# Prompt attention in 16 steps of two heads with softmax in place, and gates in quarters by tanh

## The chip, the cores and the metric

The kernel runs on one core of a Trainium2 chip. The metric is the device time of one execution in microseconds (us). Three runs of the kernel before took 1583.16, 1587.78 and 1589.92 us; the median is 1587.78.

## The reference

One decoder layer for two groups of tokens that share weights: a prompt of 512 tokens and 64 sample tokens (8 sequences of 8), 1024 channels. The layer is half a SwiGLU feed-forward (width 2816), a combined input projection that feeds a convolution branch and a sparse attention branch, a merge by two sigmoid gates, an output projection and another half feed-forward. What matters here, cut to its core:

```python
# h = rms_norm(x); q, k, v: 8 heads x 64; u: 512 channels for the convolution
gate_c, gate_a = sigmoid(gc), sigmoid(ga)              # 1024 channels each

def gathered_attention(q, k_sel, v_sel, valid):
    logits = einsum('thd,tkhd->thk', q, k_sel) * 64 ** -0.5
    logits = where(valid[:, None, :], logits, -inf)
    p = softmax(logits, axis=-1)
    return einsum('thk,tkhd->thd', p, v_sel)

def merge_branches(x, conv_out, att, gate_c, gate_a, w_aout, w_o):
    a = att.reshape(B, T, 512) @ w_aout
    return x + (gate_c * conv_out + gate_a * a) @ w_o
```

For the prompt, the keys of a token are the 128 best of the causal ones by an indexer score; for a sample token they are 256 of 4096 cached ones, gathered from HBM. The convolution is causal, depthwise and 31 wide.

## The kernel before

All is fp32. Activations lie transposed, channels on partitions and the 576 tokens (64 sample, 512 prompt) along the free dimension; 576 columns are done as two halves of 288 (HALF) in two PSUM banks. The order of work on each engine is written out by hand, and engines are tied by semaphores. DMA queues hold the weights: SP loads w_in in tiles of 512 KB into six slots (`wn`), and tile m is loaded when tile m-6 has been used (`native_load`, on the semaphore ring_used).

The stage that the change touches begins after the 14 mixing units (`mix_unit`) that compute a part of the input projection. Its parts are interleaved:

Prompt attention. 32 steps, four blocks of 128 queries times eight heads. Block b has 128 (b+1) keys. In step i TensorE computes the logits of head i (`plogits`, bank 5, contraction over the 64 rows of the head, 64 h mod 128 being the first row), VectorE adds a bias that masks the keys not selected, finds the extremum and writes to Lp (`prompt_mask`, L2495), ScalarE takes exp into Pp with the sum of the row (`pexp`, L1695), VectorE takes the reciprocal (`prompt_quotient`), ScalarE scales (`pscale`, L1701), TensorE transposes (`pturn`, L1222, bank 6) two steps later, ScalarE copies to pTp (`pevac`, L1708), TensorE multiplies by the values (`pvalue`, L1232, bank 7, 64 columns of the array) three steps after the logits, and ScalarE copies out every second head (`pout`).

Gates. The last ten weight tiles, 14 to 23, give five of the eight pairs of gate rows; each tile holds half of the contraction. `gate_half` (L1198) does 8 matmuls of 288 columns on one tile and one of two groups m of output rows, at the 20 steps of HALF_AT, into banks 0 to 3. ScalarE applies Sigmoid (`gate_low`, L1681, `gate_high`, L1686), and `save_gate` stores the 1152 columns to HBM.

Sample attention values. `values(n)` (L1094) multiplies gathered value rows of value n in four column parts of 32, into bank 4; values 11 to 31 run in steps 0 to 20. GpSimd gathers them, four indirect DMAs per value, into three buffers (`gather_values`, L2719): gather n may start when value n-3 has been used. ScalarE prepares the weights (`fill`), VectorE masks the result of each eight (`own_heads`). In step 24 come `new_values` and `group_out`, small products.

Convolution. VectorE does one of the 31 taps per step (`conv_tap`, L2530, four instructions of 512 columns) and eight pieces of the sample's (`conv_sample`). When the last is done, TensorE sums over channels (`conv_sums`, L1241, banks 1 and 2), which ends the stage; then follow the merging units (`unit`, L592) with the gates' multiplications in VectorE (`gate`), the output projection and the second feed-forward.

Of the kernel before, what the change touches and what calls it, by code (L numbers as in the profile page):

```python
# [23 lines left out]
P = 128  # L24
# [82 lines left out]
def hybrid_step(nc, inp, con, out):  # L107
    ctx = ExitStack()
    with ctx:  # L109
# [121 lines left out]
        (pTp, gpack), e_ = place(used["iT"][0], [("pTp", (P, 2, 4, P), F32), ("gpack", (P, KC, NS), F32)])  # L231
        assert e_ <= used["wisc"][0]
        (Lp, Pp, mzb), e_ = place(used["h_hi"][0], [("Lp", (P, 2, SEQ), F32), ("Pp", (P, 4, SEQ), F32), ("mzb", (P, 2, DA), F32)])
# [93 lines left out]
        STEP_0 = 11  # L327
        FILL_AT = {2 * b - STEP_0 - 2: b for b in range(7, 16)}
        HEADS_AT = {8 * g + 8 - STEP_0: g for g in range(1, 4)}
        V_SLOT, V_SEM, V_KEYS = (4, 0, 2), (4, 5, 0), (60, 62, 64)  # L330
        HALF_AT = (0, 2, 3, 4, 6, 8, 9, 10, 12, 14, 15, 16, 18, 20, 22, 24, 25, 26, 28, 30)
# [240 lines left out]
        def _(pe):  # L572
# [616 lines left out]
            def gate_half(n, m):  # L1189

                if m == 0:
                    pe.wait_ge(S_(f"ring{(NB + n) % RING}"), native_count(NB + n))
                if n % 2 == 0:
                    pe.wait_ge(S_("mix_free" if m else "sgb_ready"), n // 2 - 2)
                wt = wn[:, SLOT[(NB + n) % 6], :].rearrange("p (k n) -> p k n", k=4)
                for k in range(4):
                    for hf_ in range(2):
                        mm = pe.matmul(ps[:, 2 * m + hf_, 0:HALF], wt[:, k, m * P:(m + 1) * P],  # L1198
                                       h32[:, 4 * (n % 2) + k, hf_ * HALF:(hf_ + 1) * HALF],
                                       start=(n % 2 == 0 and k == 0), stop=(n % 2 == 1 and k == 3))  # L1200
                if m == 1:
                    mm.then_inc(S_("ring_used"), 1)
                elif n % 2 == 1:
                    mm.then_inc(S_("gate_part"), 1)

            steps = [(b, h) for b in range(4) for h in range(H)]

            def plogits(i):
                b, h = steps[i]
                r = 64 * (h % 2)  # L1210
                if i >= 1:
                    pe.wait_ge(S_("plog_used"), i)
                pe.matmul(ps[:, 5, 0:P * (b + 1)], qTp[r:r + 64, h // 2, P * b:P * (b + 1)], kTp[r:r + 64, h // 2, 0:P * (b + 1)],
                          start=True, stop=True).then_inc(S_("plog_done"), 1)

            def pturn(i):
                b, h = steps[i]
                pe.wait_ge(S_("pprob_ready"), i + 1)
                if i >= 1:
                    pe.wait_ge(S_("pturn_evac"), i)  # L1220
                for kb in range(b + 1):
                    mm = pe.transpose(ps[:, 6, kb * P:(kb + 1) * P], Pp[:, i % 4, kb * P:(kb + 1) * P], ident[:, :])  # L1222
                mm.then_inc(S_("pturn_done"), 1)

            def pvalue(i):
                b, h = steps[i]
                r = 64 * (h % 2)
                pe.wait_ge(S_("pturn_evac"), i + 1)
                if i >= 2 and i % 2 == 0:
                    pe.wait_ge(S_("patt_evac"), i // 2)  # L1230
                for kb in range(b + 1):
                    mm = pe.matmul(ps[r:r + 64, 7, 0:P], vnp[:, kb, h * HD:(h + 1) * HD], pTp[:, i % 2, kb, :],  # L1232
                                   start=(kb == 0), stop=(kb == b))
                mm.then_inc(S_("patt_done"), 1)
# [9 lines left out]
            for i in range(len(steps) + 3):  # L1244
                if i < len(steps):
                    plogits(i)
                if i in HALF_AT:
                    q = HALF_AT.index(i)
                    gate_half(N_MIX + q // 2, q % 2)
                if 2 <= i <= len(steps) + 1:  # L1250
                    pturn(i - 2)
                if i >= 3:
                    pvalue(i - 3)
                if i + STEP_0 < 32:
                    values(i + STEP_0)
                if i == 24:
# [4 lines left out]
                if i == 34:  # L1261
                    pe.wait_ge(S_("mix_free"), 10)
                    conv_sums(0, yacc)
# [24 lines left out]
        def _(act):  # L1288
# [295 lines left out]
            def sigmoid(half):  # L1584

                for m in range(2):
                    act.activation(halves(sgb[:, m, :]), pair_ps(half, m), ACT.Sigmoid).then_inc(S_("sgb_ready" if m == 0 else "mix_free"), 1)  # L1587
# [33 lines left out]
            def save_gate(i):  # L1621

                act.wait_ge(S_("sgb_ready"), i + 3)
                act.wait_ge(S_("mix_free"), i + 3)
# [52 lines left out]
            def gate_low(i):  # L1677

                act.wait_ge(S_("gate_part"), i - 2)
                act.wait_ge(S_("gate_saved"), 16 * i + 16)  # L1680
# [36 lines left out]
            for i in range(35):  # L1717
                if i < 32:
                    pexp(i)
# [1104 lines left out]
```

## Time and profile before

| | |
|---|---|
| median of three runs | 1587.78 us (1583.16 to 1589.92) |
| span of the profiled execution | 1586.6 us |
| PE (TensorE) | 1484.6 us busy, 94% |
| DVE (VectorE) | 1104.5 us, 70% |
| ACT (ScalarE) | 499.6 us, 31% |
| POOL (GpSimd) | 585.4 us, 37% |
| read from and written to HBM | 237.58 MB and 10.20 MB |

The profile is of one execution. Busy time of an engine is the union of its instructions; waits on semaphores aren't in it. Starts of matmuls are recorded, their ends are modelled. PEld is the loading of weights into the array. The granted clock is a share of 2.4 GHz. A releaser is inferred from semaphore events; "issue" means that no releaser was found, "remote" that it wasn't an engine's instruction that the trace can name.

### The profile page before, as it was taken

What the parts mean: (1) busy time and instruction counts of PE and PEld (TensorE: products, weight loads), DVE (VectorE), ACT (ScalarE), POOL (GpSimd) and SP (SyncE); (2) the same over time, 40 slices, a digit from 0 to 9 for tenths busy, and PEclk for the clock granted to TensorE, in tenths of its full rate; (3) what the DMA queues carried; (4) which work ended last, traced back from release to release, by engine and by line L of the source; (5) the groups of instructions that cost most, each with busy time, mean ns of one, the idle gap of its engine ahead of it and who ended that gap; (6) DMA issues with size and microseconds to landing.
All of it is one profiled execution on the core that took longest, in us unless ns stands there. A gap on an engine that the chain in (4) does not pass through costs nothing. (4 is left out here: it accounts for less than half of the span.)

```text
span 1586.6 us, 20793 instructions
## 1 busy us (share of the span) xinstructions
PE 1484.6 (94%) x8219; PEld 1147.5 (72%) x8219; DVE 1104.5 (70%) x1680; ACT 499.6 (31%) x756; POOL 585.4 (37%) x412
## 2 busy tenths in 40 slices
PE   5989999899999989999899789999999999999998
PEld 2323488677888865446666445669999999999998
DVE  1357399999985898999996676565679865565221
ACT  2233322112112222121212344464346544453221
POOL 2001264443338865554245775013120645520000
PEclk9998999999999999999999898999999999999999
DMA  9994153222226888868458776023422332222222
GB/s 343 389 381 161 50 85 113 93 80 80 80 80 221 286 276 276 290 213 278 125 163 269 222 237 187 17 101 126 138 75 68 93 107 82 92 68 74 74 87 93
DMA packets 156931, 248.77 MB, mean 157 GB/s; under 512 B 11965, under 2 KB 104909, under 8 KB 156571
## 3 DMA queue, kind: packets, MB, share of 16 engines
q1 hardware_dynamic: 131742, 164.22, 32.0%
q0 software_dynamic: 23104, 76.16, 15.4%
q10 hardware_dynamic: 1989, 7.07, 1.1%
q8 instruction: 64, 1.05, 0.3%
q14 instruction: 32, 0.26, 0.0%
HBM read 237.58 MB, written 10.20 MB: 156 GB/s over the span
## 5 line engine op out<-in xcount | busy, mean ns | idle before, releaser
L2651 POOL TENSOR_TENSOR w_lo<-w_raw,w_hi 128x1024 fp32r<-128x1024 f32 x65 | 165.5, 2546 | 294.8 <-ACT w_hi L1303 294.6
L686 PE MATMUL ps<-bh,wqr 128*128 128x288 f32 x936 | 205.3, 295 | 4.2 <-DVE wqr L1843 2.0
L1303 ACT ACTIVATE w_hi<-w_raw 128x1024 fp32r<-128x1024 f32 x88 | 91.5, 1040 | 314.7 <-PE ps L637 231.5
L2707 POOL DMA_INDIRECT kv<-cache_k,idxT x128 | 142.2, 1111 | 81.4 <-DVE kprod L2356 48.9
L2719 POOL DMA_INDIRECT kv<-cache_v,idxT x128 | 134.7, 1052 | 99.3 <-PE ps L1094 47.0
L686 PEld LDWEIGHTS ps<-bh,wqr 128*128 128x128 f32 x936 | 155.5, 188 | 5.0 <-DVE wqr L1843 3.9
L637 PE MATMUL ps<-h_hi,w_hi 128*128 128x512 f32 x352 | 139.2, 395 | 2.8 <-POOL w_lo L2651 1.5
L637 PE MATMUL ps<-h_lo,w_hi 128*128 128x512 f32 x352 | 137.7, 391 | 0.0
L637 PE MATMUL ps<-h_hi,w_lo 128*128 128x512 f32 x352 | 137.7, 391 | 0.0
L1079 PE MATMUL ps<-h,wn 128*128 128x288 f32 x448 | 115.5, 417 | 8.1 <-ACT sgb L1587 4.6
L702 PE MATMUL ps<-a_hi,wqr 128*128 128x288 f32 x704 | 122.3, 295 | 0.0
L686 PE MATMUL ps<-bl,wqr 128*128 128x288 f32 x384 | 113.3, 295 | 0.0
L1079 PEld LDWEIGHTS ps<-h,wn 128*128 128x128 f32 x448 | 86.2, 195 | 37.0 <-ACT sgb L1587 6.2
L1044 PE MATMUL ps<-wn,xg 128*128 128x512 f32 (+1 forms) x256 | 103.2, 563 | 5.0 <-DVE xT L2175 3.0
L702 PEld LDWEIGHTS ps<-a_hi,wqr 128*128 128x128 f32 x704 | 103.1, 188 | 0.0
L1856 DVE TENSOR_TENSOR wqr<-wq,wqr 128x1024 fp32r<-128x1024 f32 (+1 forms) x24 | 27.2, 1135 | 95.2 <-ACT wqr L1341 95.2
L1044 PEld LDWEIGHTS ps<-wn,xg 128*128 128x128 f32 x256 | 49.7, 196 | 56.2 <-issue 47.1
L1198 PE MATMUL ps<-h,wn 128*128 128x288 f32 x320 | 88.3, 432 | 0.7 <-ACT sgb L1686 0.7
L2356 DVE TENSOR_TENSOR kprod<-kv,qb 128x1024 f32<-128x1024 f32 x64 | 81.9, 1280 | 8.5 <-issue 3.1
L2775 POOL TENSOR_TENSOR wq<-wq 128x1024 f32<-128x1024 f32 x10 | 24.9, 2490 | 170.4 <-PE ps L686 76.7
L637 PE MATMUL ps<-a1h,w_hi 128*128 128x512 f32 x176 | 71.6, 407 | 14.8 <-DVE w_lo L1812 7.5
L1198 PEld LDWEIGHTS ps<-h,wn 128*128 128x128 f32 x320 | 62.6, 201 | 27.2 <-issue 8.7
(493 smaller groups left out, 3268.9 us busy)
## 6 DMA issues: line engine op xcount, KB each, us to landing
w_raw<-w_ffn_in SPq DMA_DIRECT2D x56, 512.0 KB, 13.1
wq<-w_ffn_in SPq DMA_DIRECT2D x40, 512.0 KB, 3.6
wn<-w_in SPq DMA_DIRECT2D x36, 512.0 KB
qb<-q_scratch SPq DMA_DIRECT2D x64, 256.0 KB
ring<-w_ffn_in SPq DMA_DIRECT2D x28, 512.0 KB
w_raw<-w_ffn_out SPq DMA_DIRECT2D x24, 512.0 KB, 10.1
wq<-w_ffn_out SPq DMA_DIRECT2D x20, 512.0 KB
ring<-w_ffn_out SPq DMA_DIRECT2D x14, 512.0 KB
```

Source lines behind the costliest of these rows:

```text
L637: mm = pe.matmul(ps[:, 2 * half + m, :], w[:, k, m * P:(m + 1) * P], x[:, kc0 + k, c0:c0 + SEQ], start=(first and k == 0 and fst), stop=(l ...
L686: mm = pe.matmul(ps[:, bank + m, 0:HALF], w[:, k, m * P:(m + 1) * P], b[:, j, k, :], start=(j in (0, 1, 5) and k == 0 and fst), stop=(k == ...
L702: mm = pe.matmul(ps[:, 4 * half + 2 * m + hf_, 0:HALF], w[:, k, m * P:(m + 1) * P], x[:, kc0 + k, hf_ * HALF:(hf_ + 1) * HALF], start=(kc0 ...
L1044: mm = pe.matmul(ps[:, s % 8, 0:n], xg[:, kk, P * b:P * b + P], wt[:, k, :], start=(kk == 0), stop=(kk == KD - 1))
L1079: mm = pe.matmul(ps[:, 4 * half + 2 * m + hf_, 0:HALF], wt[:, k, m * P:(m + 1) * P], h32[:, 4 * (n % 2) + k, hf_ * HALF:(hf_ + 1) * HALF], ...
L1198: mm = pe.matmul(ps[:, 2 * m + hf_, 0:HALF], wt[:, k, m * P:(m + 1) * P], h32[:, 4 * (n % 2) + k, hf_ * HALF:(hf_ + 1) * HALF], start=(n % ...
L1303: act.activation(w_hi[:, slot, 0:n], w_raw[:, slot, 0:n], ACT.Copy).then_inc(S_("hi_ready"), 1)
L1856: dve.tensor_tensor(wqr[:, 6 + o % 2, 0:n], wq[:, 8 + o % 2, 0:n], wqr[:, 4 + o % 2, 0:n].bitcast(F32), ALU.subtract).then_inc(S_("lo_read ...
L2356: dve.tensor_tensor(kprod[:, :, :], kv[:, n % KV, :, :], qb[:, j, :].unsqueeze(1).to_broadcast([P, 2, DA]), ALU.mult)\
L2651: pool.tensor_tensor(w_lo[:, slot, 0:n], w_raw[:, slot, 0:n], w_hi[:, slot, 0:n].bitcast(F32), ALU.subtract)\
L2707: pool.indirect_dma_start(kv[:, n % KV, c, :], None, rows[0], bass.IndirectOffsetOnAxis(ap=idxT[:, c, n:n + 1], axis=0))\
L2719: pool.indirect_dma_start(kv[:, V_SLOT[j % 3] + a // 2, a % 2, :], None, rows[1], bass.IndirectOffsetOnAxis(ap=idxT[:, j % 2, t:t + 1], ax ...
```

## The change

The prompt attention goes in 16 steps of two heads. Logits of the two heads are issued one behind the other, on rows 0 to 63 and 64 to 127 of the array, into banks 5 and 6. Mask, exp and scaling all work in one buffer, Pp, with three places of two heads; Lp is gone. The two value products alternate between columns 0 to 63 and 64 to 127 for each block of keys. Transposes go to banks 2 and 3. TensorE's order in a step is logits j, values j-2, one gate quarter, transposes j-1, the other quarters of the step, sample values. Two convolution taps are done per step.

Gates are computed in quarters, 8 matmuls over the whole contraction for one of two groups of rows and one half of the columns, from both tiles of a pair, alternately into banks 0 and 1; the last is in step 13. ScalarE applies tanh(x/2) in the place of the sigmoid, in all eight pairs. The merge restores it: (tanh + 1) times the branch, and a factor 0.5 in the splitting of the merged rows.

```diff
-        STEP_0 = 11
+        QUARTERS = ((0, 1), (2,), (3,), (4, 5), (6,), (7,), (8, 9), (10,), (11,), (12, 13), (14,), (15,), (16, 17), (18, 19))
+        VALUES = ((11, 12), (13,), (14, 15), (16,), (17, 18), (19,), (20, 21), (22,), (23,), (24, 25), (26, 27), (28,), (29, 30), (31,))
...
+            def gate_quarter(q):
+
+                n, m, hf_ = N_MIX + 2 * (q // 4), q % 4 // 2, q % 2
+                if q % 4 == 0:
+                    for t in (n, n + 1):
+                        pe.wait_ge(S_(f"ring{(NB + t) % RING}"), native_count(NB + t))
+                if q < 2:
+                    pe.wait_ge(S_("mix_free"), 5)
+                else:
+                    pe.wait_ge(S_("gate_taken"), q - 1)
+                for k in range(KD):
+                    wt = wn[:, SLOT[(NB + n + k // 4) % 6], :].rearrange("p (k n) -> p k n", k=4)
+                    mm = pe.matmul(ps[:, hf_, 0:HALF], wt[:, k % 4, m * P:(m + 1) * P], h32[:, k, hf_ * HALF:(hf_ + 1) * HALF],
+                                   start=(k == 0), stop=(k == KD - 1))
+                    if q % 4 == 3 and k % 4 == 3:
+                        mm.then_inc(S_("ring_used"), 1)
...
+            def plogits(j):
+
+                b, hp = j // 4, j % 4
+                nk = P * (b + 1)
+                if j >= 1:
+                    pe.wait_ge(S_("plog_used"), 2 * j)
+                for h in range(2):
+                    r = 64 * h
+                    mm = pe.matmul(ps[:, 5 + h, 0:nk], qTp[r:r + 64, hp, P * b:P * (b + 1)], kTp[r:r + 64, hp, 0:nk], start=True, stop=True)
+                mm.then_inc(S_("plog_done"), 1)
...
+                for kb in range(b + 1):
+                    for h in range(2):
+                        r = 64 * h
+                        mm = pe.matmul(ps[r:r + 64, 7, 0:P], vnp[:, kb, (2 * hp + h) * HD:(2 * hp + h + 1) * HD], pTp[:, (2 * j + h) % 3, kb, :],
+                                       start=(kb == 0), stop=(kb == b), skip_group_check=True)
...
+            for j in range(18):
+                if j < 16:
+                    plogits(j)
+                if j >= 2:
+                    pvalue(j - 2)
+                if j < len(QUARTERS):
+                    gate_quarter(QUARTERS[j][0])
+                if 1 <= j <= 16:
+                    pturn(j - 1)
+                if j < len(VALUES):
+                    for q in QUARTERS[j][1:]:
+                        gate_quarter(q)
+                    for n in VALUES[j]:
+                        values(n)
+                if j == 14:
+                    pe.wait_ge(S_("mz_ready"), 4)
+                    new_values()
...
+                if j == 17:
+                    pe.wait_ge(S_("gate_taken"), 20)
+                    pe.wait_ge(S_("pturn_evac"), 32)
                     conv_sums(0, yacc)
```

ScalarE and VectorE:

```diff
-                sigmoid(0)
+                sigmoid(0, ACT.Tanh, 0.5)
...
+                act.activation(sgb[:, m, hf_ * HALF:(hf_ + 1) * HALF], ps[:, hf_, 0:HALF], ACT.Tanh, scale=0.5).then_inc(S_("gate_taken"), 1)
...
+            for j in range(18):
+                if 1 <= j <= len(QUARTERS):
+                    for q in QUARTERS[j - 1]:
+                        gate_evac(q)
+                if j == 2:
                     act.wait_ge(S_("kv_out"), 16 * 12)
+                if j >= 2:
+                    pout(j - 2)
+                if j < 16:
+                    pexp(2 * j)
+                    pexp(2 * j + 1)
+                if 1 <= j <= 16:
+                    pevac(2 * j - 2)
+                    pevac(2 * j - 1)
+                if j < 16:
+                    pscale(2 * j)
+                    pscale(2 * j + 1)
...
-                dve.wait_ge(S_("plog_done"), n + 1)
+                if n % 2 == 0:
+                    dve.wait_ge(S_("plog_done"), n // 2 + 1)
+                    if n >= 6:
+                        dve.wait_ge(S_("pturn_done"), n - 4)
...
+            for j in range(16):
+                if j in HEADS_AT:
+                    own_heads(HEADS_AT[j])
+                if j == 2:
+                    dve.wait_ge(S_("unat_out"), 32)
+                for h in range(2):
+                    prompt_mask(j // 4, 2 * j + h, (2 * j + h) % 4)
...
+                conv_tap(2 * j)
+                for h in range(2):
+                    prompt_quotient(2 * j + h, (2 * j + h) % 4)
+                if j < 15:
+                    conv_tap(2 * j + 1)
+                if j < 8:
+                    conv_sample(j // 2, j % 2)
...
-                    ins = dve.tensor_tensor(halves(g[:, m, :]), halves(g[:, m, :]), pair_ps(1 - v % 2, m), ALU.mult)
+                    ins = dve.scalar_tensor_tensor(out=halves(g[:, m, :]), in0=halves(g[:, m, :]), scalar=1.0, in1=pair_ps(1 - v % 2, m), op0=ALU.add, op1=ALU.mult)
```

## Rows read from the trace of the kernel before

**Rows 1.** The page: the span, and TensorE's busy time with its share and instructions.
```profile
span 1586.6 us, 20793 instructions
...
PE 1484.6 (94%) x8219; PEld 1147.5 (72%) x8219; DVE 1104.5 (70%) x1680; ACT 499.6 (31%) x756; POOL 585.4 (37%) x412
```

**Rows 2.** Stretches: length, busy time and instructions of each engine, clock, DMA, GB/s.
```profile
868.90:1063.41 194.51, 175.52 (x844) 107.71 (x840) 128.64 (x255) 86.26 (x184) 84.85 (x81) 0.93 0.50 153
...
950.00:960.00 10.00, 9.14 (x31) 5.23 (x32) 8.89 (x16) 2.82 (x9) 6.83 (x7) 0.66 0.60 172
```

**Rows 3.** Waits from 868.9 to 1063.41: who for whom, us, times, longest.
```profile
DVE Lp L2495 <- PE ps L1213: 30.2, 11, 7.6
DVE Lp L2495 <- remote: 23.3, 9, 5.8
```

**Rows 4.** Timeline, TensorE: start, length (us), line, tiles, shapes, count.
```profile
961.25 0.70 PE L1213 MATMUL ps<-kTp,qTp 64*128 64x256 f32 x2
961.87 4.15 PE L1198 MATMUL ps<-h,wn 128*128 128x288 f32 x16
965.86 0.38 PE L1222 MATMUL ps<-ident,Pp 128*128 128x128 f32 x2
966.17 0.65 PE L1232 MATMUL ps<-pTp,vnp 128*64 128x128 f32 x4
966.75 1.06 PE L1094 MATMUL ps<-kv,zq 128*32 128x512 f32 x8
967.74 0.91 PE L1213 MATMUL ps<-kTp,qTp 64*128 64x384 f32 x2
```

**Rows 5.** Timeline, TensorE, near the end of the stage.
```profile
1052.46 0.60 PE L1222 MATMUL ps<-ident,Pp 128*128 128x128 f32 x4
1052.99 1.09 PE L1232 MATMUL ps<-pTp,vnp 128*64 128x128 f32 x8
1054.01 1.12 PE L1213 MATMUL ps<-kTp,qTp 64*128 64x512 f32 x2
1055.07 0.66 PE L1222 MATMUL ps<-ident,Pp 128*128 128x128 f32 x4
```

**Rows 6.** Timeline, TensorE, from the small products to the logits behind them.
```profile
1014.58 0.68 PE L1130 MATMUL ps<-pnT,vns 64*64 64x64 f32 x16
...
1019.26 1.22 PE L1213 MATMUL ps<-kTp,qTp 64*128 64x512 f32 x1
```

**Rows 7.** Timeline, TensorE: indexer logits of four heads on 32 rows each.
```profile
668.40 0.71 PE L1021 MATMUL ps<-iT 32*128 32x256 f32 x8 [0.73 <-ACT iT L1557]
```

**Rows 8.** Timeline, VectorE: masks (L2495), taps (L2530), sample convolution (L2538).
```profile
873.46 0.27 DVE L2495 CUSTOM_DVE_ANT_0 Lp<-ps,causal 128x128 f32<-128x128 f32 x1
...
942.47 1.19 DVE L2538 TENSOR_TENSOR G<-U_s,wconv 128x992 f32<-128x992 f32 x1
...
945.15 0.41 DVE L2495 CUSTOM_DVE_ANT_0 Lp<-ps,bias_new 128x256 f32<-128x256 f32 x1
...
945.49 2.74 DVE L2530 SCALAR_TENSOR_TENSOR yacc<-U_p,wconv,yacc 128x512 f32<-128x512 f32 x4
...
1046.08 0.69 DVE L2495 CUSTOM_DVE_ANT_0 Lp<-ps,bias_new 128x512 f32<-128x512 f32 x1 [0.52 <-PE ps L1213]
```

**Rows 9.** Timeline: GpSimd's gathers and two waits of TensorE's sample values.
```profile
872.34 0.94 POOL L2719 DMA_INDIRECT kv<-cache_v,idxT  x1 [0.30 <-issue]
...
877.75 1.32 PE L1094 MATMUL ps<-kv,zq 128*32 128x512 f32 x8 [2.87 <-issue]
...
950.86 1.93 PE L1094 MATMUL ps<-kv,zq 128*32 128x512 f32 x8 [2.85 <-issue]
```

**Rows 10.** Groups by form, ScalarE, 868 to 1056: count, busy us, mean ns, idle.
```profile
L1695 ACT ACT_TABLE_LOAD x10 | 12.8, 1283 | 6.7 <-issue 5.2 <-ACT sgb L1686 1.5
...
L1695 ACT ACTIVATE Pp<-Lp,small 128x384 f32<-128x384 f32 x8 | 4.9, 616 | 12.5 <-DVE small L2495 12.5
```

**Rows 11.** Timeline, TensorE: the first convolution sums and their wait.
```profile
1063.41 0.75 PE L1241 MATMUL ps<-yacc,ones 128*128 128x288 f32 x2 [0.87 <-ACT sgb L1686]
```

More of the change, by code:

```diff
@@ L1187, in _ @@
             pe.wait_ge(S_("us_state"), 3 + 2 * KC)
[L1189 to L1203, printed above, removed]
-                    mm.then_inc(S_("gate_part"), 1)
@@ L1225, in pvalue @@
[L1225 to L1233, printed above, removed]
+            def gate_quarter(q):
[13 more added lines that the diff above has]
+                        mm.then_inc(S_("ring_used"), 1)
+                if q % 4 < 3:
+                    mm.then_inc(S_("gate_part"), 1)
@@ L1583, in _, with sigmoid @@
                     act.activation(dst[:, b, :], ps[:, (4 * g + b) % 8, 0:n], ACT.Copy, scale=rcol[:, b:b + 1]).then_inc(S_("nat_evac"), 1)
-            def sigmoid(half):
+            def sigmoid(half, func=ACT.Sigmoid, scale=1.0):
                 for m in range(2):
-                    act.activation(halves(sgb[:, m, :]), pair_ps(half, m), ACT.Sigmoid).then_inc(S_("sgb_ready" if m == 0 else "mix_free"), 1)
+                    act.activation(halves(sgb[:, m, :]), pair_ps(half, m), func, scale=scale).then_inc(S_("sgb_ready" if m == 0 else "mix_free"), 1)
             def fill(b):
@@ L1621, in save_gate @@
             def save_gate(i):
-                act.wait_ge(S_("sgb_ready"), i + 3)
-                act.wait_ge(S_("mix_free"), i + 3)
+                if i < 3:
+                    act.wait_ge(S_("sgb_ready"), i + 3)
+                    act.wait_ge(S_("mix_free"), i + 3)
+                else:
+                    act.wait_ge(S_("gate_taken"), 4 * (i - 2))
                 act.dma_start(gate_dram[i:i + 1, :, :].rearrange("o p n -> p (o n)"), sgb[:, :, :].rearrange("p m n -> p (m n)"))\
@@ L2573, in _ @@
                     dve.wait_ge(S_("us_state"), 2 * KC + 1)
[L2574 to L2578 removed]
+                conv_tap(2 * j)
+                for h in range(2):
+                    prompt_quotient(2 * j + h, (2 * j + h) % 4)
[3 more added lines that the diff above has]
+                    conv_sample(j // 2, j % 2)
+                if j == 15:
                     sample_heads()
@@ L2606, in gate @@
                         dve.wait_ge(S_("parts_hi"), KA + KC + 2 * (v - 4) + m + 1)
-                        dve.tensor_tensor(m_lo[:, 2 * (v - 4) + m, :], g[:, m, :], m_hi[:, 2 * (v - 4) + m, :].bitcast(F32), ALU.subtract)\
+                        dve.scalar_tensor_tensor(out=m_lo[:, 2 * (v - 4) + m, :], in0=g[:, m, :], scalar=0.5, in1=m_hi[:, 2 * (v - 4) + m, :].bitcast(F32), op0=ALU.mult, op1=ALU.subtract)\
                             .then_inc(S_("m_ready"), 1)
```

142 lines of the change are left out of this document (50 added, 92 removed).

## The prediction

> **What bounds the kernel now.** The page says where to look: TensorE (PE) is busy 94% of the span of 1586.6 us [rows 1], so time comes out where PE has less to do or waits less. The change touches only the prompt-attention stage, which PE enters with the first logits at 868.90 us and leaves when the convolution sums start at 1063.41. The table of stretches shows 194.51 us there, PE busy 175.52, so 19.0 us idle, and a mean granted clock of 0.93 [rows 2]. The clock has two levels, 2.4 and 1.2 GHz; a mean of 0.93 is 14% of the stage, 27 us, at the lower one, where each us does half a us of work: 13.6 us lost. One low stretch is seen between 950 and 960, where the mean is 0.66 [rows 2]. VectorE (DVE) is busy 128.64 of the 194.51, ScalarE (ACT) 86.26, GpSimd (POOL) 84.85 [rows 2]: none fills the stage, but DVE is next. After the stage PE goes on to matmuls of prepared weights that it runs nearly without a gap, so I count a stage shortened by x as a kernel shortened by x. DVE waits with its mask for PE's logits 30.2 us in 11 waits, and 23.3 us in 9 more whose releaser the trace doesn't name [rows 3]: the engines hand small tasks to and fro 32 times.
>
> **PE's work before, by starts.** Ends of matmuls are modelled, so I price each piece from its start to the next start. From the middle of the stage [rows 4]: logits of 256 keys 0.62 us (961.25 to 961.87), half a gate 3.99, two transposes 0.31, values of two key blocks 0.58, sample values 0.99. From its end [rows 5]: four transposes 0.53, values of four blocks 1.02, logits of 512 keys 1.06. So 128 more keys cost 0.22 in logits, 0.22 in values and 0.11 in transposes, whose start alone costs 0.09. Each block of queries has eight heads:
> logits 8 x (0.40+0.62+0.84+1.06) = 23.4; values 8 x (0.36+0.58+0.80+1.02) = 22.1; transposes 8 x (0.20+0.31+0.42+0.53) = 11.7; gates 20 x 3.99 = 79.8; sample values 11 to 31, 21 x 0.99 = 20.8; the small products of new_values and group_out 4.7 (1014.58 to 1019.26) [rows 6]. Sum 162.5. With 13.6 of clock and 19.0 idle that is 195.1 against the measured 194.5: the account closes.
>
> **The change, part by part.** *Two heads at once.* The two logits use rows 0 to 63 and 64 to 127 and go to banks 5 and 6; the two value products use columns 0 to 63 and 64 to 127 of one bank. The trace has both kinds of side-by-side work: four matmuls of 32 rows and 256 keys (an fp32 matmul shows as two records) took 0.71 us together [rows 7], as much as the one of 64 rows (0.70) [rows 4], and the sample values, four column parts of 512 elements, take 0.99 in all [rows 4], about one alone. So I price a pair as one head: logits 4 x 2.92 = 11.7 (-11.7), values 4 x 2.76 = 11.0 (-11.1). The bounds are 0 and the full halves. Transposes use the whole array and only share their start: 4 x (0.31+0.53+0.75+0.97) = 10.2 (-1.5). Gates in quarters are the same 8 matmuls per piece, 79.8; sample values 20.8 (seven follow another directly and may be 0.1 shorter, not counted); small products 4.7. Sum 138.2, which is 24.3 less.
>
> *Waits, by walking the 16 steps.* PE's step j is logits j, values j-2, a gate quarter, transposes j-1, the other quarters, sample values; by the prices above 9.8, 5.7, 6.9, 9.9, 7.1, 6.5, 11.4, 6.7, 6.9, 11.9, 8.2, 7.4, 12.2, 11.6, 7.9 (with the small products), 3.3, 2.2 and 1.0 us. Logits j+1 need DVE's two masks of step j, transposes j the scaling in ACT of step j, with a whole step between. DVE's step is two masks (0.41 us at 256 keys, 0.69 at 512), two taps at 2.74 and in the first eight steps one sample convolution with its reciprocal, 2.68 from 942.47 to the next mask at 945.15 [rows 8]: 8.7 to 9.0 us in the first eight steps, 6.3 to 6.9 later. It starts at 873.46, as before, after the last key selection [rows 8], and passes 943 to 944 us at the start of step 8, where PE asks for logits 9 at about 943: 1 us of wait. From there PE has more per step. POOL issues a value's four gathers at 0.94 us each with 0.30 between, 5.0 us at best [rows 9], and I take 5.3, and a gather may start only when the value three before it is used. Value 12's last gather ended at 873.28 and PE started value 12, after 2.87 idle, at 877.75: 4.4 us of landing [rows 9]. With that, value 12 now comes after two quarters and is there; value 15 comes right behind 14 at 890.9 but lands at about 894 (3.3 us of wait); value 27 costs 1.4. At the end transposes 15 wait for DVE's tap 30 and the scaling behind it, 2.9. Idle by the walk 8.5. Before, several of the 19.0 have no cause I can name (the 23.3 us of unnamed releasers are their other side [rows 3]); handshakes are halved and most have slack, so I add 3: 11.5 instead of 19.0 (-7.5). Bounds: 8.5 and 19.
>
> *The clock.* The low stretch after 950 came with a wait of 2.85 us at 950.86, and the wait at 877.75 was as long [rows 2, 9]. A wait of this length remains at value 15, one at the end, and the small products with 16 columns stay. I take 10 of 13.6 (-3.6); bounds 3 and 13.6, with nothing measured that would make it worse, since PE idles less.
>
> *Tanh for sigmoid, banks of their own.* ACT loads its function table ten times ahead of exp, at 1283 ns each [rows 10], and as often on the way back to sigmoid: 25.7 us of an engine 44% busy. The convolution sums wait 0.87 us for the last sigmoid [rows 11]. The last quarter now runs in step 13, so this goes; it is in the idle sum above. Whether tanh and exp share a table no row shows. If they do, ACT loses all but at most one load and nothing more falls on the path, because PE does not wait for exp in the walk.
> The Trainium skill says that they do: "ScalarE: Activation LUTs", section "Table sets: the hidden batching unit", lists tanh in the set of exp, and also in that of sigmoid; no run here shows it yet.
>
> *Edits at nothing.* A quarter waits for ACT's copy two quarters back (gate_taken); transposes and sample values are queued behind it, but the copy is at the head of ACT's previous or present step. Weights: a tile of the pair is released at the fourth quarter, so SP's loads of tiles 36 and 37 start at about 889 instead of right behind the halves, for use at 944; the cover is 50 us. Tile 31 is wanted at 869 instead of 887; its load is issued during the mixing units, ahead of the stage. DVE's wait for transposes three steps back, and for unat_out in step 2, is for work long done. Merging gains 24 scalar_tensor_tensor in place of tensor_tensor; a tap of that form on 512 elements takes 0.69 us, as does the mask that reads PSUM [rows 8], so the form costs little: 0 to 0.1 us each, beside PE's units, 0 to 1 us in all.
>
> The sum: -24.3 - 7.5 - 3.6 = -35.4. Of the profiled 1586.6 that leaves 1551.2; the median of the runs, 1587.78, is 1.2 above the span, so 1552 us.
>
> **The rivals.**
> 1. *Waits and clock stay as they were* (32.6 us): only the work goes, 1563. For it: part of the idle has no named cause. Against: fewer, slacker handshakes.
> 2. *DVE becomes the bound.* Its work is 15.4 in masks, 84.9 in 31 taps, 21.4 in samples, some 3 in the rest, 125 us from 873.5, ending at 998; if it still waited the 53.5 us that the masks wait now [rows 3], the stage would end near 1052: 12 saved, 1576. Against: it lags behind PE in the first nine steps and has nothing to wait for.
> The Trainium skill has this as a rule: "TensorEngine Tiling (Array Packing)", section "PSUM Bottleneck", says that tiling speeds up TensorE but not the emptying of PSUM, which may become the limit; before the change the trace shows no such limit, with DVE busy for 66% of the stage.
> 3. *The row halves don't overlap*: 11.7 back, 1564. [rows 7] speaks against it.
> 4. *Tanh has another table than exp*: two loads at each of 14 groups of quarters, 36 us of ACT; half of them ahead of exp, 18 us, of which slack hides two thirds: 6 on the path, 1558.
> 5. *The walk holds exactly* and the clock loses 3: -24.3 - 10.5 - 10.6, 1542.
> 6. *Slower: the step's chain is not hidden.* With ACT's passes at the 0.62 us of exp on 384 keys [rows 10]: logits 0.84, masks 1.1, exp 0.6, the tap ahead of the reciprocal 2.9, scaling 1.2, transposes 0.75, copy 0.6, values 0.8, 8.8 us. If the in-order queues left only gates and sample values (100.6 in 16 steps, 6.3 each) outside it, a step would take 15.1 us and sixteen 242, against 194.5: 1635. It decides from 12.2 us per step. The order by code puts one step between mask and transposes and another before the values, which speaks against.
>
> **How the numbers follow.** Forecast 0.50; rival 1 0.17; 2 0.08; 3 0.04; 4 0.06; 5 0.11; 6 0.04. 1552 is the likeliest case; alone it would span 1546 to 1559. The range 1537 to 1571 takes in rivals 1, 3, 4 and 5 and leaves out 2 and 6. About 0.5% (8 us) is what a measurement can tell from no change: faster than 1580 in all cases but 6 and the worst of 2, so 0.94; within 0.02; slower 0.04.
>
> **What would show it.** Pairs of logits of 512 keys at about 1.1 us from start to next start, value pairs of four blocks at 1.0: else rival 3. No or one table load in the stage: else rival 4. The convolution sums start at 1025 to 1030 with PE idle 10 to 13 us and a mean clock of 0.93 to 0.96. A wait at value 15 near 891. Masks that wait for logits in the first nine steps would show DVE ahead, not behind. Wrong would be: PE idle over 19 us, or a stage that ends later than 1040.

## The result, and the profile after

The changed kernel takes 1549.12 us (median of 4 runs, 1545.92 to 1551.51), the kernel before beside it 1585.68 us (4 runs, 1583.16 to 1589.92). The ratio is 0.976, with a 95% interval of 0.9736 to 0.9788. Forecast were 1552 us and a range of 1537 to 1571. The page of the changed kernel, span and busy time, as [rows 1]:

```profile
span 1548.8 us, 20748 instructions
...
PE 1459.2 (94%) x8219; PEld 1136.7 (73%) x8219; DVE 1101.8 (71%) x1680; ACT 472.6 (31%) x746; POOL 586.4 (38%) x412
```

PE is busy 25.4 us less, by as many matmuls. The table of stretches (columns as in [rows 2]) for the stage, for the only two stretches in it with a lower clock, and for what follows the stage:

```profile
869.49:1024.11 154.62, 141.90 (x845) 91.18 (x841) 126.25 (x256) 58.98 (x174) 87.01 (x81) 0.98 0.64 204
890.00:900.00 10.00, 6.83 (x36) 3.07 (x35) 9.86 (x19) 2.79 (x11) 6.83 (x7) 0.83 0.94 328
1010.00:1020.00 10.00, 9.01 (x77) 7.41 (x76) 9.17 (x21) 6.48 (x15) 2.43 (x1) 0.83 0.71 269
1024.11:1204.00 179.89, 172.10 (x1222) 167.89 (x1220) 131.88 (x122) 83.69 (x110) 43.03 (x17) 0.98 0.30 98
```

The stage went from 194.5 to 154.6 us, which is 39.9 less; it starts 0.6 later, and the rest of the kernel behind it takes 524.7 us instead of 523.2; so the span falls by 37.8. A mean clock of 0.83 over 10 us is 3.4 us at 1.2 GHz instead of 2.4, which costs half of it, 1.7; the two stretches together cost 3.4 us. Behind the stage, in the stretch with 0.98, the clock is low twice for about 3.4 us, from 1127.6 and from 1199.6; the kernel before has no low clock from 1063 to 1250.

TensorE's pieces from the timeline, to be read from start to next start, as [rows 4], [rows 5] and [rows 6]: pairs of 256, 384 and 512 keys, a wait at a sample value, waits at values, and the end of the stage:

```profile
895.50 1.88 PE L1096 MATMUL ps<-kv,zq 128*32 128x512 f32 x8 [3.17 <-DMA kv<-cache_v,idxT]
...
908.00 0.70 PE L1218 MATMUL ps<-kTp,qTp 64*128 64x256 f32 x4
908.64 0.44 PE L1244 MATMUL ps<-pTp,vnp 128*64 128x128 f32 x4
...
963.37 0.92 PE L1218 MATMUL ps<-kTp,qTp 64*128 64x384 f32 x4
964.21 0.88 PE L1244 MATMUL ps<-pTp,vnp 128*64 128x128 f32 x12
...
1006.87 1.13 PE L1218 MATMUL ps<-kTp,qTp 64*128 64x512 f32 x4
1007.93 1.09 PE L1244 MATMUL ps<-pTp,vnp 128*64 128x128 f32 x16
1008.95 1.09 PE L1232 MATMUL ps<-ident,Pp 128*128 128x128 f32 x8
1009.97 0.68 PE L1132 MATMUL ps<-pnT,vns 64*64 64x64 f32 x16
1010.59 1.96 PE L1105 MATMUL ps<-qsel,mz 128*128 128x16 f32 x16
1012.39 1.94 PE L1105 MATMUL ps<-qsel,mzb 128*128 128x16 f32 x16
...
1020.23 1.09 PE L1244 MATMUL ps<-pTp,vnp 128*64 128x128 f32 x16 [1.22 <-ACT pTp L1726]
...
1023.08 1.09 PE L1244 MATMUL ps<-pTp,vnp 128*64 128x128 f32 x16 [0.74 <-ACT pTp L1726]
1024.11 1.24 PE L1253 MATMUL ps<-yacc,ones 128*128 128x288 f32 x4
```

A pair of logits of 512 keys takes 1.06 us (1006.87 to 1007.93) and a pair of values of four blocks 1.02 (1007.93 to 1008.95), each as much as one head in [rows 5], though it has twice the records. The convolution sums at 1024.11 have no wait in brackets; in [rows 11] they waited for the last sigmoid.

Waits of the changed kernel from 868 to 1030 (who for whom, us, times, longest), as [rows 3]:

```profile
DVE Pp L2515 <- remote: 7.0, 3, 3.8
...
PE ps L1244 <- ACT pTp L1726: 6.7, 4, 2.4
...
DVE Pp L2515 <- PE ps L1218: 5.2, 4, 2.0
...
PE ps L1096 <- DMA kv<-cache_v,idxT: 3.7, 2, 3.2
...
PE ps L1203 <- issue: 2.2, 5, 0.7
```

DVE's 53.5 us of waits at its masks became 12.2. PE's three lines make 12.6 us, the whole of its idle time. Groups by form of ScalarE from 868 to 1056, as [rows 10]: the tanh copies, and the first table load in that stretch, which belongs to the square root of the convolution's norm, behind the stage:

```profile
L1704 ACT ACTIVATE sgb<-ps 128x288 f32<-128x288 f32 x20 | 7.7, 402 | 8.3 <-remote 6.6 <-PE ps L1203 1.7
...
L1773 ACT ACT_TABLE_LOAD x1 | 1.3, 1283 | 0.0
```

### The profile page after: what moved, and what is told of

It reads as the page before. It is cut to its first block and busy times, and to the rows that moved or that the text cites. A ratio compares the mean times of both kernels' runs of the same rounds, so it can differ in the third digit from the quotient of the medians.

```text
span 1548.8 us, 20748 instructions
## 1 busy us (share of the span) xinstructions
PE 1459.2 (94%) x8219; PEld 1136.7 (73%) x8219; DVE 1101.8 (71%) x1680; ACT 472.6 (31%) x746; POOL 586.4 (38%) x412
## 5 line engine op out<-in xcount | busy, mean ns | idle before, releaser
L1318 ACT ACTIVATE w_hi<-w_raw 128x1024 fp32r<-128x1024 f32 x88 | 91.5, 1040 | 316.7 <-PE ps L639 234.2
L1081 PE MATMUL ps<-h,wn 128*128 128x288 f32 x448 | 115.7, 418 | 5.6 <-issue 2.2
L1081 PEld LDWEIGHTS ps<-h,wn 128*128 128x128 f32 x448 | 86.6, 195 | 34.5 <-issue 5.9
L1046 PE MATMUL ps<-wn,xg 128*128 128x512 f32 (+1 forms) x256 | 106.5, 578 | 4.9 <-DVE xT L2192 2.4
L1203 PE MATMUL ps<-h,wn 128*128 128x288 f32 x320 | 83.7, 412 | 2.3 <-issue 2.2
L2376 DVE TENSOR_REDUCE G<-kprod 128x16 f32<-128x1024 f32 x64 | 78.2, 1221 | 2.2
## 6 DMA issues: line engine op xcount, KB each, us to landing
w_raw<-w_ffn_in SPq DMA_DIRECT2D x56, 512.0 KB, 12.7
```

The source lines that it names most:

```text
L1046: mm = pe.matmul(ps[:, s % 8, 0:n], xg[:, kk, P * b:P * b + P], wt[:, k, :], start=(kk == 0), stop=(kk == KD - 1))
L1081: mm = pe.matmul(ps[:, 4 * half + 2 * m + hf_, 0:HALF], wt[:, k, m * P:(m + 1) * P], h32[:, 4 * (n % 2) + k, hf_ * HALF:(hf_ + 1) * HALF], ...
L1203: mm = pe.matmul(ps[:, hf_, 0:HALF], wt[:, k % 4, m * P:(m + 1) * P], h32[:, k, hf_ * HALF:(hf_ + 1) * HALF], start=(k == 0), stop=(k == K ...
L1318: act.activation(w_hi[:, slot, 0:n], w_raw[:, slot, 0:n], ACT.Copy).then_inc(S_("hi_ready"), 1)
L2376: dve.tensor_reduce(G[:, :, n], kprod[:, :, :].rearrange("p c (h d) -> p (c h) d", h=H), AX.X, ALU.add).then_inc(S_("logits_ready"), 1)
```

## The experiments

The table gives the same account for each kernel. Stage: from the first prompt logits to the convolution sums. Idle: the stage less PE's busy time. Clock: half of the time at the lower level. Work: what is left. The ratio is that to the kernel before, run beside it; before had a median of 1569.4 us beside e1 to e4, 1574.1 beside e5 to e8, and 1585.2 beside e10 to e12, so times are compared between these groups by their ratios only. Each group ran on another chip; the changed kernel ran with the second (e5) and in its first measurement, not beside e1 to e4 or e10 to e12, so stages compared across groups below are worth less than those within one.

The columns overlap where the clock is low while PE waits: that time is in idle and again in clock, and work is too short by as much. In stretches of half a us it makes 1.1 us in before, 1.0 in e9, 0.8 to 1.2 in e3, e7 and e8, 2.2 in e12, 3.3 in e11, and nothing in the others. With it work is 162.9 in before and in e9, as in e1, and 137.4 and 137.0 in e11 and e12, whose edits took no work away.

| kernel | stage | idle | clock | work | ratio, 95% interval |
|---|---|---|---|---|---|
| before | 194.5 | 19.0 | 13.6 | 161.9 | 1 |
| e9, before again | 192.0 | 16.5 | 13.7 | 161.8 | one run, 1589.5 us |
| changed | 154.6 | 12.7 | 3.4 | 138.5 | 0.976 (0.9736 to 0.9788) |
| e5, changed again | 145.7 | 6.5 | 1.7 | 137.5 | 0.974 (0.9717 to 0.9769) |
| e1, tanh in before | 178.0 | 8.2 | 6.9 | 162.9 | 0.998 (0.9967 to 0.9991) |
| e2, sigmoid in changed | 145.4 | 6.1 | 1.7 | 137.6 | 0.978 (0.9760 to 0.9796) |
| e3, logits apart | 161.2 | 4.4 | 10.2 | 146.6 | 0.986 (0.9845 to 0.9878) |
| e4, values apart | 150.2 | 6.4 | 3.4 | 140.4 | 0.980 (0.9786 to 0.9818) |
| e6, values later | 149.0 | 5.2 | 5.1 | 138.7 | 0.974 (0.9720 to 0.9762) |
| e7, values moved | 151.2 | 8.5 | 6.8 | 135.9 | 0.979 (0.9765 to 0.9809) |
| e8, e6 and e7 | 151.2 | 8.6 | 5.1 | 137.5 | 0.979 (0.9760 to 0.9809) |
| e10, no pairs | 179.5 | 8.3 | 11.9 | 159.3 | 0.992 (0.9894 to 0.9951) |
| e11, groups late | 164.2 | 17.0 | 13.2 | 134.0 | 0.981 (0.9785 to 0.9837) |
| e12, late and spread | 170.0 | 18.7 | 16.5 | 134.8 | 0.986 (0.9834 to 0.9882) |

### e9 and e5: the two kernels again

Neither has an edit.

> The kernel before, unchanged, for its trace: where it runs on the chip of the runs from tanh alone on, its stage is at hand beside theirs. By theory W its parts are as first seen: work by starts of 162 us, and above it idle time and low clock, which may be smaller than the 19.0 and 13.6 us of the first trace, since the kernel before with tanh alone shows a stage of 178.0 us with 8.2 idle and 6.9 lost to the clock. I expect a stage of 180 to 188.

> The changed kernel unchanged, beside the next three on one chip. Its ratio should be 0.976 again, and its trace shows what of the idle time and of the low clock is the same from one execution to the next: the waits at sample value 15 (3.2 us) and of the value products for the copies (6.7 us) by theory W the same within 1 us, the low stretches anywhere.

The stretch of the stage, e9 first:

```profile
872.42:1064.46 192.04, 175.55 (x844) 108.85 (x840) 128.44 (x255) 86.78 (x184) 83.85 (x81) 0.93 0.51 159
```

```profile
862.36:1008.06 145.70, 139.19 (x845) 90.65 (x841) 124.87 (x255) 58.33 (x174) 89.74 (x81) 0.99 0.68 217
```

The ratio repeats. Work is the same to 1 us in both executions of each kernel, while idle and clock of the changed kernel are 8 us lower in e5. Both expectations missed: e9's stage is 192.0 and not 180 to 188, and in e5 the wait at value 15 is 1.85 us instead of 3.17, those for ScalarE's copy 3.5 instead of 6.7. e5 ran on a chip on which the kernel before took 1574.1 us, against 1585.7 beside the first measurement; whether chip or execution makes the difference isn't separated. So one execution's idle and clock are good to some us only, and the differences read below from these two columns alone are weak where they are smaller than that.

### e1 and e2: tanh alone, and all but tanh

e1 puts tanh into the kernel before and changes the merge with it; e2 takes both out of the changed kernel.

```diff
e1 (before)
-                sigmoid(0)
+                sigmoid(0, ACT.Tanh, 0.5)
e2 (changed)
-                act.activation(sgb[...], ps[:, hf_, 0:HALF], ACT.Tanh, scale=0.5).then_inc(S_("gate_taken"), 1)
+                act.activation(sgb[...], ps[:, hf_, 0:HALF], ACT.Sigmoid).then_inc(S_("gate_taken"), 1)
```

> The kernel before with only the tanh part of the change: gates as tanh(x/2), restored in the merge, steps and halves as before. Theory W (the gain is TensorE's work and its waits; ACT's table loads lie beside them): the 20 loads of the stage go or all but one, which is 25.7 us less in ACT, and the kernel gains 0 to 3 us (the wait of 0.87 us at the convolution sums and some of the idle time): 1583 to 1587 where the kernel before has 1586. Theory L (the loads held the hand-over between the engines, and that is a main part of the gain): at least half of the ten loads ahead of exp, 6 us or more, 1579 or less. If tanh has another table than exp, 20 loads stay and the time stays.

> The changed kernel with sigmoid in place of tanh, all else as changed. 14 groups of quarters now need two loads each, up to 28 loads of 1.28 us, 36 us more in ACT. Theory W: ACT is busy 59 of 155 us in the stage, but value products already wait for ACT's copies of the transposes (6.7 us), so some of it shows: 2 to 8 us, 1551 to 1557. Theory L: half of the loads (those ahead of exp) and more on the path: 18 us or more, 1567.

e1 gains 3.4 us of 1569.4, an effect between 0.1 and 0.3%. e2 brings the table loads back. ScalarE's groups from 855 to 1040 us of e2, and its stage:

```profile
L1712 ACT ACT_TABLE_LOAD x15 | 19.2, 1283 | 4.9 <-DVE small L2515 4.7
L1704 ACT ACT_TABLE_LOAD x14 | 18.0, 1283 | 0.2
```

```profile
862.73:1008.11 145.38, 139.29 (x844) 90.68 (x840) 125.46 (x255) 97.55 (x203) 89.80 (x81) 0.99 0.69 217
```

29 loads take 37.2 us of ScalarE, and the stage is as long as without them (145.4 against e5's 145.7, on another chip). e2's own trace says why: behind a load ahead of exp ScalarE mostly still waits for VectorE's mask (0.99 us at 919.78, 1.19 at 928.65), and PE waits for a copy of a gate once:

```profile
925.74 4.15 PE L1203 MATMUL ps<-h,wn 128*128 128x288 f32 x16 [0.85 <-ACT sgb L1704]
```

So nearly all of the loads lies beside TensorE's work. The ratio is 0.35% above e5's, with intervals that overlap. Tanh is worth 0 to 6 us, of which the stage shows at most this 0.85.
The Trainium skill, "ScalarE: Activation LUTs", section "Table sets: the hidden batching unit", says that tanh lies in the set of exp; the changed kernel shows it, with no load between 20 tanh copies and 32 exp in turn, where sigmoid has 29.

### e3, e4 and e10: the pairs undone

In e3 the values of the pair before stand between the two logits of a step; in e4 the value products go head after head instead of in turn; e10 does both apart, so that of the change the 16 steps, the quarters and tanh are left.

```diff
e3
                 if j < 16:
-                    plogits(j)
+                    plogits(j, 0 if j >= 2 else None)
                 if j >= 2:
                     pvalue(j - 2)
+                if 2 <= j < 16:
+                    plogits(j, 1)
e4
-                for kb in range(b + 1):
-                    for h in range(2):
+                for h in range(2):
+                    for kb in range(b + 1):
e10 (one half of each at a time)
+                    plogits(j, 0 if j >= 2 else None)
+                    pvalue(j - 2, 0)
+                    plogits(j, 1)
+                    pvalue(j - 2, 1)
```

> The changed kernel with the second head's logits issued behind the value products instead of right behind the first head's, from step 2 on, so that the two row halves never run side by side. Theory W: the 14 pairs cost their second part again, 2 x 0.40 + 4 x (0.62 + 0.84 + 1.06) = 10.9 us, and a change of tile more per step, about 12 in all: 1559 to 1563. Rival H (the gain is that the engines meet 16 times instead of 32, with the idle time and the clock that follow): 0 to 3 us, 1549 to 1552.

> The changed kernel with the value products of one head's key blocks first and then the other's, instead of in turns, so that the column halves meet only at the seam. Theory W: 0.22 us for each key block but one of the second head, 4 x (0+1+2+3) x 0.22 = 5.3 us if the seam overlaps, 4 x (1+2+3+4) x 0.22 = 8.8 if it doesn't: 1554 to 1558. Rival H: 0 to 2 us, 1549 to 1551.

> The changed kernel with no two halves side by side: per step from 2 on, logits of one head, its value products, logits of the other, its value products. 16 steps, banks, buffers, order of the other engines and tanh are kept. Theory W: 10.9 us for the logits, 4 x 2.76 = 11.0 for the values and two changes of tile more per step, 2 to 4: 24 to 26 us of TensorE's work come back, and a few us of low clock with it as in the run with the logits apart: 0.976 + 0.016 to 0.019, a ratio to the kernel before of 0.991 to 0.996. Rival H (16 meetings instead of 32 are worth most): 0.985 or less.

Timeline of TensorE in e3, one step's logits of 384 keys:

```profile
956.47 0.91 PE L1218 MATMUL ps<-kTp,qTp 64*128 64x384 f32 x2
957.31 0.88 PE L1245 MATMUL ps<-pTp,vnp 128*64 128x128 f32 x12
958.11 0.91 PE L1218 MATMUL ps<-kTp,qTp 64*128 64x384 f32 x2
958.95 4.15 PE L1203 MATMUL ps<-h,wn 128*128 128x288 f32 x16
```

One head takes 0.84 us here (956.47 to 957.31), and so does the pair in the changed kernel (963.37 to 964.21). Fourteen steps of it are 9.1 us of work against e5; idle is lower, and the clock costs 8.5 more. e2, which ran beside e3 and e4 on one chip and differs from the changed kernel by the sigmoid alone, is a check: e3 is 14.7 us slower than it (1548.4 against 1533.7), e4 4.4 (1538.1).

Timeline of TensorE in e4, values of four blocks, head after head:

```profile
990.35 1.58 PE L1244 MATMUL ps<-pTp,vnp 128*64 128x128 f32 x16
991.86 1.09 PE L1232 MATMUL ps<-ident,Pp 128*128 128x128 f32 x8
```

1.51 us, where in turn it takes 1.02 and two single heads 2.04 [rows 5]. Head after head keeps half of the gain at four blocks, more than I had expected, and it makes e4 the smaller effect: stage 4.5 longer than e5's, work 2.9 of it, where 5.3 to 8.8 were expected.

The stage of e10, a stretch:

```profile
871.07:1050.54 179.47, 171.16 (x845) 107.36 (x841) 125.11 (x255) 58.92 (x174) 85.88 (x81) 0.93 0.56 176
```

e10 gains 0.8%, some 12 us of 1585: against e9 the stage has 2.5 less work, 8.2 less idle and 1.8 less clock (some 3.5 and 0.8 for work and clock, with the overlap of the columns counted once). The pairs are the other 1.6%, some 25 us: against the changed kernel 20.8 of work and 8.5 of clock, with 4.4 less idle. So two thirds of the gain come with the pairs: work side by side, and the lower clock that goes with undoing it. The other third comes from all the rest together: 16 steps, quarters, transposes of two heads in a row, and tanh, which alone is 0.2% (e1). That fewer handshakes are the main part of it is argued and not shown; e1's stage, on another chip, has only 8.2 us idle too, with 32 steps.

### e6, e7 and e8: the waits that are left

e6 has the values behind the first quarter, so that ScalarE's copy of the transposes has longer; e7 spreads the values otherwise: 15 goes a step later, away from 14, and so do 18 and 27; e8 does both.

```diff
e6
-                if j >= 2:
-                    pvalue(j - 2)
                 if j < len(QUARTERS):
                     gate_quarter(QUARTERS[j][0])
+                if j >= 2:
+                    pvalue(j - 2)
e7
-VALUES = ((11, 12), (13,), (14, 15), (16,), (17, 18), (19,), ..., (26, 27), (28,), (29, 30), (31,))
+VALUES = ((11, 12), (13,), (14,), (15, 16), (17,), (18, 19), ..., (26,), (27, 28), (29, 30), (31,))
```

> The changed kernel with the value products of step j-2 behind the first gate quarter of step j instead of ahead of it: 4 us more for ACT's copies, which wait behind exp, which waits for DVE's mask. Theory W (those waits are real and stand on the path): the 4.7 us at steps 5 and 10 go, the two at the end (2.0) have no quarter behind which to hide and stay: 3 to 5 us less, 1544 to 1547. Rival: what was waited there is waited at the transposes or at the logits, whose masks DVE gives late: no change, 1549.

> The changed kernel with the sample values spread otherwise over the steps: 15 moves from step 2 to 3, 18 from 4 to 5, 27 from 10 to 11, so that none comes ahead of its gather by the walk. Theory W: the wait of 3.2 us at value 15 goes and the low clock behind it (3.4 us at half clock, 1.7) may go too: 3 to 5 us less, 1544 to 1547. Rival (DVE, 7 to 9 us per step in the first nine steps, is then the bound): PE waits for masks or copies instead, no change, 1549.

> Both edits, value products later and sample values spread otherwise. Theory W: they add up, 6 to 9 us less than the changed kernel, 1540 to 1543. Rival: DVE's steps sum to 80 us in the first nine and PE meets them there, so that the two together bring no more than one, 1545.

e6 was to gain 3 to 5 us and changed nothing: 0.974 as e5. Two of the four waits for ScalarE's copy went, but in e5 they were small (four waits, 3.5 us in all), and the clock cost 3.4 more. e7 was to gain as much and is slower than e5 by 0.4%; their runs don't overlap. Its timeline of TensorE at the two values:

```profile
894.70 1.07 PE L1096 MATMUL ps<-kv,zq 128*32 128x512 f32 x8
901.98 1.93 PE L1096 MATMUL ps<-kv,zq 128*32 128x512 f32 x8 [6.21 <-DVE mz L2528]
```

Value 15 is there at 894.70. Value 16 begins a new sum in the same bank and needs own_heads to have taken values 8 to 15 out of it; in VectorE's queue that stands at the start of the next step, behind two taps and a sample convolution of this one, and it began at 901.24. PE waits 6.21 us, and is at 1.2 GHz behind it (1.93 for the eight matmuls that take 1.07 ahead of it). A wait of 2 to 3 us on a DMA (1.85 in e5, 3.17 in the changed kernel) was traded for one of 6 on VectorE. e8 has the same, 6.78 us.

### e11 and e12: the small products at the end

new_values and group_out (64 and 16 columns per matmul) go from step 14 to step 16, where PE waits for the last copies; e12 also spreads the values more and puts the last tap behind the last quotients.

```diff
e11
+                if j == 16:
+                    pe.wait_ge(S_("mz_ready"), 4)
+                    new_values()
+                    for g in range(4):
+                        group_out(g)
                 if 1 <= j <= 16:
                     pturn(j - 1)
...
-                if j == 14:
-                    pe.wait_ge(S_("mz_ready"), 4)
-                    new_values()
-                    for g in range(4):
-                        group_out(g)
e12, with e11's
-VALUES = ((11, 12), (13,), (14, 15), (16,), (17, 18), (19,), ..., (26, 27), (28,), (29, 30), (31,))
+VALUES = ((11, 12), (13,), (14,), (15,), (16, 17), (18, 19), ..., (26,), (27, 28), (29, 30), (31,))
-                conv_tap(2 * j)
+                if j < 15:
+                    conv_tap(2 * j)
                 for h in range(2):
                     prompt_quotient(2 * j + h, (2 * j + h) % 4)
+                if j == 15:
+                    conv_tap(30)
```

> The changed kernel with the small products (new_values, group_out, 4.3 us) moved from step 14 to step 16, ahead of the last transposes, where PE waits 1.7 and 0.7 us for ACT's copies. Theory W: these waits hide behind them, 2 to 3 us less, a ratio of 0.973 beside 0.974 to 0.976 of the changed kernel. Rival: VectorE then adds the sample heads later and the merge waits for them, 0 to 2 us more.

> The same, and two edits more: the sample values spread so that 15 stands alone in step 3 and 16 with 17 in step 4 (value 16 had waited 6.2 us for VectorE where it stood behind 15 in one step), and the last reciprocals ahead of tap 30. Theory W: the wait of 1.9 to 3.2 us at value 15 goes too, and the low clock behind it where there was one: 4 to 6 us less than the changed kernel, a ratio of 0.971 to 0.973. Rival: PE meets VectorE's masks instead in the first nine steps, no gain over the run before it.

e11 was to gain 2 to 3 us and e12 4 to 6; both are slower than the changed kernel, e11 by 0.5% (the intervals just touch) and e12 by 1.0%. The timeline of e11 with ScalarE and VectorE, some rows left out, from the transposes of step 15 on:

```profile
1010.00 1.27 PE L1232 MATMUL ps<-ident,Pp 128*128 128x128 f32 x8 [0.21 <-ACT Pp L1719]
...
1011.81 0.68 DVE L2515 CUSTOM_DVE_ANT_0 Pp<-ps,bias_new 128x512 f32<-128x512 f32 x1
...
1012.53 0.72 ACT L1712 ACTIVATE Pp<-Pp,small 128x512 f32<-128x512 f32 x1 [0.87 <-DVE small L2515]
...
1013.96 1.06 ACT L1726 ACTIVATE pTp<-ps 128x512 f32<-128x512 f32 x2
```

```profile
1015.07 1.98 PE L1244 MATMUL ps<-pTp,vnp 128*64 128x128 f32 x16 [3.80 <-ACT pTp L1726]
1016.98 1.12 PE L1132 MATMUL ps<-pnT,vns 64*64 64x64 f32 x16
1018.03 3.59 PE L1105 MATMUL ps<-qsel,mz 128*128 128x16 f32 x16
1021.46 3.57 PE L1105 MATMUL ps<-qsel,mzb 128*128 128x16 f32 x16
```

The transposes are done by 1011.3, but ScalarE's queue has the copy behind two exp, and these behind the masks, which VectorE reaches at 1011.81 behind a tap: PE gets its operand at 1015.07. In the changed kernel the small products stand a step earlier (1009.97 to 1014.26), ahead of the last logits; ScalarE and VectorE go on meanwhile, and the same wait is 1.22 us (at 1020.23). The new place could hide neither wait: it is behind this one, and the last values (1023.08 in the changed kernel, 0.74; 0.69 in e11) wait for a copy of transposes that themselves come behind the small products. The stretch from the wait to the end of the stage:

```profile
1015.17:1029.41 14.24, 13.55 (x88) 12.37 (x89) 2.44 (x7) 2.69 (x5) 0.00 (x0) 0.50 0.12 38
```

All of its 14.2 us are at 1.2 GHz, which costs 7.1 (the clock was low from 1013.2, inside the wait); half of group_out, 1.80 us in the changed kernel (1010.59 to 1012.39), take 3.43 (1018.03 to 1021.46). The work that was moved took its cover with it and ran at half speed. Not all of e11's loss need be this: waits of 3.38 us at 894.13 and 6.45 at 979.36 have another origin (last section), and the six runs of e11 spread from 1548.6 to 1558.4. e12 has the same wait of 3.81 and the same 3.43 us at its end. Its other spreading of the values did remove the wait for VectorE of e7, but one of 3.48 us for a gather came at 924.66.

No version tried beats the changed kernel; e6 equals it.

## Why the prediction was right, and where it was off

**Work, right.** 138.2 us were forecast, 138.5 measured (137.5 in e5). (The steps of the walk add up to 136.6, as step 0 stands with 9.8 where its own prices give 10.4; that shifts the walk's meetings a little and not the sum.) The pairs cost what one head costs, and each kind was shown by itself: 0.84 us for one head in e3 and for two in the changed kernel; 1.51 head after head in e4 against 1.02 in turn in the changed kernel. The bound of full halves, and with it rival 3, is excluded. Eight transposes took 1.02 (1008.95 to 1009.97) against a forecast of 0.97.

**Idle, right in sum, not in its parts, and in part by luck.** 11.5 forecast, 12.7 measured, but 6.5 in e5. The wait at value 15 was 3.3 at about 891 to 894, and is 3.17, ending at 895.50. The tail was to cost 2.9 and costs 1.96 (1.22 and 0.74). The waits at value 27 (1.4) and at step 9's logits (1.0) did not come; in their place are two waits for ScalarE's copy of 2.4 us each, which the walk did not have and which only the 3 us without a name covered. In e5 idle is below the forecast's lower bound of 8.5; there the wait at step 9's logits did come, on VectorE's mask as forecast, and that at value 27 was 0.15:

```profile
937.78 0.92 PE L1218 MATMUL ps<-kTp,qTp 64*128 64x384 f32 x4 [0.98 <-DVE small L2515]
```

The 53.5 us that VectorE waited with its masks [rows 3] fell to 12.2, as halved handshakes with slack were to do, and e10 has this part without the pairs: 8 us less idle than e9. That the handshakes did it is not shown by itself. Rival 1 (waits stay) fell.

**The clock, the term that was mis-sized.** 10 us were to remain of 13.6; 3.4 remained in the stage, 1.7 in e5. I took the number of waits of 3 us as a guide and kept most of the loss because the small products stay. They cost two stretches of 3.4 us at the lower level, one behind the wait at value 15 and one behind the small products. The term was taken as separate from the others, and it isn't: where a kernel has a longer wait (e7, e11, e12) or more, smaller pieces (e3, e10), the clock column is 3 to 13 us above the changed kernel's. Waits alone don't order it: e3 has the least idle time of all, 4.4 us, and loses 10.2; e8 waits 6.78 us at once and loses 5.1; and in e5 the one low stretch follows the small products, ahead of which PE had worked without a wait from 957.84 on. What sets the number and length of the low stretches stays open. The step put 6.6 us too much into the sum. Against it stand 1.5 behind the stage (the two low stretches there cost 3.4), 0.6 ahead of it, 1.2 more idle, 0.3 more work, and 0.6 by which my account of the stage before was too long (it counted 1.1 us of low clock during waits twice): 2.4 us are left, the difference between the span forecast, 1551.2, and the one measured, 1548.8.

**VectorE, not the bound.** 125 us of work were counted, 126.25 are busy. Its mask reached step 8 at 947 and not at 943, and was behind PE until then but for one wait of 1.7; later it waits for PE (the longest, 3.8, at 974.77), 12.2 us in all. Rival 2 and the slower case, rival 6, whose chain would have shown as waits of ScalarE's copy in every step, fell: there are four. Of rival 5 (the walk exact, clock 3) the clock's part came, the idle time's didn't.
The rule of the Trainium skill on emptying PSUM ("TensorEngine Tiling (Array Packing)", section "PSUM Bottleneck") did not decide here, with VectorE busy for 82% of the stage.

**Tanh, right.** No table load in the stage. e2 shows more: rival 4's price of 6 us was too high too, since 29 loads cost the stage at most the one wait of 0.85. Of e1's 3.4 us two waits of PE for sigmoids have a row, the last one's 0.87 [rows 11] and 0.69 at 1030.21 of the kernel before; e1 has neither. The rest has none.

**The signs.** Convolution sums at 1025 to 1030: 1024.11, a miss by 0.9. Idle 10 to 13: 12.7. Clock 0.93 to 0.96: 0.98, the other miss, and the cause of the first. Edits at nothing (weights' release, the two banks, the form of the merge): no wait of PE in the stage names SP's loads or the gates' copies; only five waits of 2.2 us in all, at quarters, have no releaser.

## What to carry to other kernels

On rows 0 to 63 and 64 to 127, or in column halves of one bank, two fp32 heads cost TensorE what one costs, if their matmuls are issued side by side; this is priced exactly from starts in the trace. All else in the change, with fewer and larger steps in it, gave a third of the gain; how much each part of it gave was not separated. Ahead of moving small work, look at what wait it covers: here three moves (e7, e11, e12) that were to remove a small wait opened a larger one, and the lower clock in and behind it cost as much again or more.

## What the runs showed of the hardware that was not expected

**Engines released late and together.** In e11 PE waits 6.45 us at 979.36. The rows before it, in the timeline of all engines:

```profile
970.03 0.82 PE L1232 MATMUL ps<-ident,Pp 128*128 128x128 f32 x6
...
978.43 0.87 ACT L1726 ACTIVATE pTp<-ps 128x384 f32<-128x384 f32 x2 [5.70 <-remote]
...
978.81 0.95 POOL L2742 DMA_INDIRECT kv<-cache_v,idxT  x1 [2.42 <-remote]
978.82 0.69 DVE L2515 CUSTOM_DVE_ANT_0 Pp<-ps,bias_new 128x512 f32<-128x512 f32 x1 [3.24 <-remote]
```

By the records the transposes began at 970.03 and took 0.82. ScalarE's copy waits for them and for values at 965.24, yet starts at 978.43, and GpSimd and VectorE, which wait for later work of PE, start within 0.4 us of it. The changed kernel has the same, 3 us behind transposes of 969.00, and it is the source of its wait of 2.37 at 974.89:

```profile
972.92 0.49 ACT L1726 ACTIVATE pTp<-ps 128x384 f32<-128x384 f32 x1 [6.32 <-remote]
```

The copy at 893.63 of e11 looks alike, 7 us behind transposes of 886.46, and gives the wait of 3.38 at 894.13. In e11 the granted clock is 0.50 from 976 on, within the recorded wait, which fits matmuls that had run when the records say; but whether they ran later than their records, or the release came late, the trace can't say for certain; no experiment was made on it. It stays open, and it is a good part of the idle time that is left.

**Column halves overlap even head after head.** 1.51 us for two heads of four blocks, against 1.02 in turn and 2.04 for two apart.

**The same work, two executions.** Work agrees to 1 us between e5 and the first execution of the changed kernel, on another chip, idle and clock differ by 8 us, and the stage starts 7 us earlier. The ratios, 0.974 and 0.976, don't show it, since the kernel before is faster there too, by 11.6 us.
